# Leaving out the twenty unread transposes ahead of the norms and of some sums, in a two-block transformer kernel

## The reference

```python
def first_block(x, ...):
    for l in range(DEPTH):          # DEPTH = 2
        x = x + 0.5 * swiglu(rmsnorm(x, ffn1_norm[l]), ffn1_w_in[l], ffn1_w_out[l])
        x = x + hybrid_mixer(rmsnorm(x, mix_norm[l]), w_in[l], ...)   # gated delta rule + stick-breaking attention
        x = x + 0.5 * swiglu(rmsnorm(x, ffn2_norm[l]), ffn2_w_in[l], ffn2_w_out[l])

def second_block(x, mem, ...):
    for l in range(DEPTH):
        x = x + hybrid_mixer_2(rms_norm(x, mix_norm[l]), ...)          # MLA + GQA attention + gMLP
        x = x + memory_cross_attention(rms_norm(x, mem_x_norm[l]), mem, ...)
        x = x + conv_gated_ffn(rms_norm(x, ffn_norm[l]), ...)
    return rms_norm(x, final_norm)
```

## Time and profile before

| | us |
|---|---|
| median of three runs | 2601.81 |
| the profiled execution | 2607.15 |
| its span, first to last instruction | 2605.3 |
| TensorE matmuls busy | 2448.4 (94%) |
| TensorE weight loads busy | 2292.1 (88%) |
| GpSimd busy | 1790.0 (69%) |
| ScalarE busy | 1115.8 (43%) |
| VectorE busy | 948.4 (36%) |
| mean granted TensorE clock, share of full | 0.973 |

### The profile page before, as it was taken

The page is one execution under the profiler, slowest core; times in us unless marked ns, Lnnn a source line. Parts: engine busy times, 40 slices in busy tenths (PEclk is TensorE's granted clock), DMA queues, the critical chain, the costliest instruction groups (busy, mean ns, idle before and its releaser), DMA issues.

```text
span 2605.3 us, 45928 instructions
## 1 busy us (share of the span) xinstructions
PE 2448.4 (94%) x17692; PEld 2292.1 (88%) x17692; DVE 948.4 (36%) x1554; ACT 1115.8 (43%) x1248; POOL 1790.0 (69%) x1372
## 2 busy tenths in 40 slices
PE   7999999998899999999999889999888999898998
PEld 7999888988899899888889889999788998787997
DVE  1114555322311211245543241112424564423564
ACT  4334434445333433444343634335454335454333
POOL 6998444455799789864445667996545997544996
PEclk9999999998999999999999899999899999899999
DMA  6554332323455455442233334564233555323553
GB/s 207 191 179 150 109 97 87 109 90 105 131 192 179 162 180 191 146 150 94 82 98 106 106 129 152 187 203 129 82 98 114 189 182 164 105 72 107 170 185 121
DMA packets 312052, 360.11 MB, mean 138 GB/s; under 512 B 18604, under 2 KB 290912, under 8 KB 311776
## 3 DMA queue, kind: packets, MB, share of 16 engines
q1 hardware_dynamic: 311904, 358.08, 42.4%
HBM read 357.00 MB, written 1.05 MB: 137 GB/s over the span
## 4 chain that ended last, share of the span: by engine, by line
POOL 43%; issue 26%; PE 25%; DVE 3%; ACT 2%; POOLq 0%; DVEq 0%; ACTq 0%
POOL sb_lo L458 43%; PE ps L482 21%; PE ps L911 1%; PE ps L887 1%; PE ps L799 1%; ACT sb_kT L1002 0%; ACT sb_sq L1328 0%; PE ps L524 0%; DVE sb_negmax L1802 0%; PE ps L960 0%; POOLq L453 0%; ACT sb_levels L1301 0%; PE ps L894 0%; DVE sb_kT L1745 0%; PE ps L869 0%
## 5 line engine op out<-in xcount | busy, mean ns | idle before, releaser
L458 POOL TENSOR_TENSOR sb_lo<-sb_raw,sb_hi 128x512 fp32r<-128x512 f32 x1368 | 1789.8, 1341 | 794.0 <-ACT sb_hi L991 791.8
L482 PE MATMUL ps<-sb_hT_h,sb_hi 128*128 128x256 f32 x3524 | 1026.6, 291 | 33.3 <-DVE sb_hT_l L1434 10.6
L482 PE MATMUL ps<-sb_hT_h,sb_lo 128*128 128x256 f32 x3524 | 1007.0, 286 | 0.0
L482 PE MATMUL ps<-sb_hT_l,sb_hi 128*128 128x256 f32 x3524 | 1006.6, 286 | 0.0
L991 ACT ACTIVATE sb_hi<-sb_raw 128x2048 fp32r<-128x2048 f32 x342 | 655.3, 1916 | 797.1 <-PE ps L482 792.3
L482 PEld LDWEIGHTS ps<-sb_hT_h,sb_hi 128*128 128x128 f32 x3524 | 684.5, 194 | 50.3 <-issue 31.3
L482 PEld LDWEIGHTS ps<-sb_hT_h,sb_lo 128*128 128x128 f32 x3524 | 685.3, 194 | 3.6 <-issue 1.4
L482 PEld LDWEIGHTS ps<-sb_hT_l,sb_hi 128*128 128x128 f32 x3524 | 684.6, 194 | 0.0
L482 PE MATMUL ps<-sb_hi,sb_o_h 128*128 128x512 f32 (+1 forms) x720 | 265.4, 369 | 9.9 <-DVE sb_o_l L1441 9.9
L482 PE MATMUL ps<-sb_hi,sb_o_l 128*128 128x512 f32 (+1 forms) x720 | 263.4, 366 | 0.0
L482 PE MATMUL ps<-sb_lo,sb_o_h 128*128 128x512 f32 (+1 forms) x720 | 262.7, 365 | 0.0
(11 more groups left out here) (320 smaller groups left out, 2811.0 us busy)
## 6 DMA issues: line engine op xcount, KB each, us to landing
sb_raw<-in_ffn_w_in SPq DMA_DIRECT2D x88, 1024.0 KB, 5.1
sb_raw<-in_w_in SPq DMA_DIRECT2D x78, 1024.0 KB, 5.2
sb_raw<-in_ffn_w_out SPq DMA_DIRECT2D x44, 1024.0 KB, 5.0
sb_raw<-in_ffn_w_up SPq DMA_DIRECT2D x44, 1024.0 KB, 5.1
sb_raw<-in_ffn_w_down SPq DMA_DIRECT2D x22, 1024.0 KB, 4.8
sb_raw<-in_w_out SPq DMA_DIRECT2D x16, 1024.0 KB, 5.1
sb_raw<-in_w_branch_a SPq DMA_DIRECT2D x8, 1024.0 KB, 5.1
sb_raw<-in_w_branch_b SPq DMA_DIRECT2D x8, 1024.0 KB, 5.1
```

The source lines that it names most:

```text
L458: ins = nc.gpsimd.tensor_tensor(lo[:, slot, c], raw[:, slot, c], hi[:, slot, c].bitcast(F32), ALU.subtract)
L482: ins = mm(dst, s, m, start=first and n == 0, stop=last and n == 3 * len(pairs) - 1)
```

## The change

One constant goes from 20 to 0, so that `warm` issues nothing. Everything else is as it was.

```diff
@@ -196,7 +196,7 @@
 PARTS = 4
-WARM = 20
+WARM = 0
```

## The result

The changed kernel takes 2610.32 us (median of 15 executions, 2605.38 to 2614.76) against 2603.04 us for the kernel before (15 executions beside them, 2600.39 to 2608.3). The ratio is 1.0025, with a 95% interval of 1.0017 to 1.0033: slower by some 6.5 us by the ratio, 7.3 us by the medians. The forecast was 2616 us and a range of 2602 to 2630. The sign and the mechanism hold; the size is about half of the 14 us that were forecast.

The account below looks back on a forecast made before the run. TensorE was taken as the bound, its matmuls covering 94% of the span. 62 us more at low clock x 0.26 = 16 us, less 1, is 15, taken as 14; on the median of 2601.81 that is 2616 us, range 2602 to 2630.

Parts of the forecast that it names:

- The runs lie in waits: At 17 of 18 places work behind the run still waits for another engine; some 43 us of TensorE, nearly none on the path.
- What the runs do besides: In TensorE's waits, the unread transposes keep it busy and lift or hold the clock; the long wait behind loses it.
- The page's rule: Rival: transposes at all runs do not count for the clock, so only the paid places count; 2601 us, chance 0.06.
- How often the clock would fall: At 16 places that lose their run, clock falls as in waits without runs: 62 us more at low clock.
- the ten longer waits: Ten places, 3.2 to 4.3 us from run's start to arrival; mean clock 0.944 falls to 0.746, 47.5 us more low.
- What a us at low clock costs: Behind a norm's wait, each us at low clock costs 0.26 us, with 0 and 0.44 as the ends.
- the place at 895.1: Ahead of the feed-forward part at 902.73: 6.8 us at low clock cost 1.75 us, 0.26 per us.
- The 1 us gained: Second block's first norm gains 0.7 us, second mixer's output norm in its first layer up to 0.4; together 1 us off.
- Little change: Rival: clock falls more often, mostly over waits; 40 us more low at 0.1 per us, 2605 us, chance 0.17.
- Faster: Rival: runs begun at low clock outlast arrivals by 1.1 to 2 us; leaving them out gives 2593 us, chance 0.07.
- Much slower: Rival: every place falls for 6.8 us and more, products take it all; 95 us low, 2640 us, chance 0.10.
- 14 compared waits: TensorE waits of 2.4 us and more without a run; mean clock 0.746 in eight, 0.847 in six, used for places losing runs.

Follow-up runs that it names:

- the first experiments: Follow-up kernels, each timed in five rounds beside the kernel before on the same chip; no single time is given for them as a group.
- the repeat: The changed kernel, without any run of unread transposes, timed a second time beside the kernel before: ratio 1.0019 (1.0010 to 1.0028).
- the one test of a link: Against the kernel before, the runs at the memory attention's norm and ahead of its sum left out in both layers: ratio 1.0027.
- the kernel with 40 records over eight rows: Against the kernel before, each unread transpose made a plain matmul over 8 rows instead of 128, same count, 40 recorded instructions a run: ratio 1.0251.

## Why the prediction was right, and where its size was off

**The runs lie in waits.** Right. The waits of the norms' transposes went from 20.6 + 0.7 to 44.5 + 5.4 us, the sums' waits from 1.0 and 1.9 to 5.4 and 6.3, as the runs moved out.

**What the runs do besides.** Right, and now shown: the rows that take part matter (8 rows against 128), the kind of instruction doesn't. The page's rule, that transposes don't engage full clock ("TensorE: Matmul & The Clock Gate" of the Trainium skill, Part 4), does not hold for these: with plain matmuls in place of the transposes the time is the same, 0.9995, and without either the clock is 0.967.

**How often the clock would fall.** The forecast had 62 us more at low clock. By the mean clock of 25 executions of the kernel before, from the first experiments, and 15 of the changed one, 0.976 and 0.967, it is 2 x 0.0095 x 2605 = 49 us (0.9764 and 0.9669 before rounding). In the repeat, timed side by side, it is 2 x 0.0086 x 2605 = 45 us. The likeness between waits with no run in them and the new ones overstated this, but not by much (62 us); the ten longer waits did all fall, mostly for 3.4 us and not for the 6 of those that were compared.

**What a us at low clock costs.** This is the term that was mis-sized: 0.26 taken, and 6.5 / 49 = 0.13 measured, half of it (5.0 / 45 = 0.11 in the repeat). The 0.26 came from the place at 895.1, where the low stretch of 6.8 us reached 4.4 us into the products. I read it as the usual case. But there the run had only put the fall off: it held the clock during the wait, and the clock fell when the first products came. Without a run the fall comes sooner, over the wait and the transposes, and a stretch of 3.4 us is over by the first product: 0.36 us, or 0.11 per us. The prediction expected feed-forward parts of 188.5 us; eleven of twelve in the two traces of the changed kernel stay at 187.2, and the one of 188.55 shows that the expected case does occur. In the trace of before three of six took 188.5 us and more (the first, the one at 902.73 and the last). So at some places the kernel before pays more on its products than the changed one: the first feed-forward part of layer 2, norm included, went from 196.40 to 195.76 us, and the last from 196.09 to 195.03. The prediction priced every low us alike. The ones that the runs leave behind lie on products and are dearer than the ones that come in their place, which lie mostly on waits and transposes.

**The 1 us gained.** At the second block's first norm the transposes did begin 0.7 us earlier, in the changed kernel 1.31 us behind the part before, but at low clock, and the first product came 6.30 us behind it where it was 5.43. The mixer behind it still came out 0.84 us shorter, 136.36 against 137.20, with other low stretches in it; that single trace doesn't tell how much of this is the term of the prediction.

**The rivals.** Little change (2605 us, 3 above before) lies nearer to the measured 6.5 than the forecast's 14, and its price of 0.1 is the better one. Its reason, that the first work behind a norm is paced by ScalarE and VectorE, fits the shorter wait ahead of the first product (0.71 for 1.18 us), but no run tested it by itself. Faster fell: no run of the kernel before costs enough. Much slower fell too: 45 to 49 us more at low clock and not 95.

**What stays open.** The norms' runs alone are worth 6.0 to 7.6 us and the sums' some 6.5, and both together 4.3 to 7.3 (medians and ratios of both measurements). The traces show low stretches that stand elsewhere when a run far ahead is left out (the feed-forward part behind the memory attention above), and patterns that repeat to 0.03 us between executions (the two traces of the changed kernel agree so in eight of fourteen stretches), but the one test of a link, between the memory norm and the memory sum, went against it. Why the costs don't add up is not settled. The profiled executions also stand closer together than the medians (2607.15 before, 2607.99 after), so single traces were used for places and not for sums.

## What to carry to other kernels

A filler in a wait is worth what the clock loses there, and that depends on what runs while the clock is low: ask whether the low stretch meets waits and short transposes (0.1 us per us here), a chain of dependent transposes and products (0.3 in the memory attention, 2.0 us over 6.8) or dense products (0.4). A filler that holds the clock through only the first part of a wait can move the fall onto the dense work, where it is dearer. And a filler must be shorter than its wait at low clock too, not only at full. Before you credit a filler with a low stretch that is gone from a trace, look whether it is gone without the filler in another.

## What the runs showed of the hardware

In float32 a plain matmul of 128 x 128 by 128 x 128 is recorded as two instructions and a transpose of the same shape as one; 10 plain matmuls (2.40 us; 2.49 over eight rows) take about as long as 20 transposes (2.35 us).

Matmuls with few rows don't hold the clock even where they leave TensorE no gap. The clearest case is the kernel with 40 records over eight rows. At its second feed-forward norm the run stands right behind dense products at full clock and goes on from 707.18 to 713.43 us, and the clock falls at 710.1, in the middle of it:

```profile
710.20:713.30 3.10, 3.10 (x16) 2.93 (x14) 0.79 (x2) 0.79 (x4) 0.00 (x0) 0.50 0.77 307
```

In the kernel before, five of its falls stand behind a stretch with no gap, and each of these stretches holds eight broadcasts of eight rows on L640 among products of all rows. The first:

```profile
412.35 1.12 PE L640 MATMUL ps<-sb_g_r,sb_const 8*128 8x256 f32 x4
413.31 1.02 PE L640 MATMUL ps<-sb_beta_r,sb_const 8*128 8x256 f32 x4
```

```profile
412.10:415.50 3.40, 3.40 (x21) 2.75 (x20) 3.13 (x7) 0.00 (x0) 0.33 (x1) 1.00 0.47 133
415.70:419.00 3.30, 3.30 (x16) 3.08 (x15) 0.69 (x1) 2.75 (x3) 0.48 (x1) 0.50 0.45 158
```

TensorE is busy for all of the first 3.40 us, for 1.9 of them with the broadcasts, and at 0.50 in the next. Three more such groups of eight (at 270.8, 341.9 and 1147.9) are not followed by a fall. The prediction took it that some of its 14 compared waits stand beside matmuls with few rows. The trace does not bear this out: none has the broadcasts of L640 near it, and two (at 1824.8 and 2237.4) stand right behind two matmuls of 32 rows (L847). Why those waits lost the clock for longer than the new ones is not settled.
